# Four reorderings at the stage boundaries of a two-layer mLSTM / Mamba-2 decoder step

## The reference

```
def _conv_ffn(h, buf, w_up, conv_w, conv_b, w_down):
    u = h @ w_up                                  # 2048 -> 2 x 5632
    u, buf_new = _causal_dwconv(u, buf, conv_w, conv_b)   # 3 taps; buf: the old rows
    g, val = jnp.split(u, 2, axis=-1)
    return (jax.nn.silu(g) * val) @ w_down, buf_new       # 5632 -> 2048
```

## Time and profile before

| | |
|---|---|
| three runs | 3429.54, 3431.39, 3434.74 us |
| span of the profiled execution, first to last instruction | 3425.9 us |
| time of the profiled execution as a run | not shown; its span is 5.5 us under the median of the runs |
| TensorE busy | 3279.2 us, 96% |
| VectorE, ScalarE, POOL busy | 2114.1, 1350.2, 887.6 us |
| mean granted TensorE clock | 0.957 of 2.4 GHz |
| DMA | 545.56 MB, 159 GB/s on average |

### The profile page before, as it was taken

One profiled execution on the slowest core, in us unless ns is written; L12 is line 12 of the kernel. 1 busy time (PEld: TensorE's weight loads), 2 busy tenths in 40 slices (PEclk: granted clock), 3 DMA queues, 4 the chain that ended last, 5 costly groups with the idle time before them and its releaser, 6 DMA issues.

```text
span 3425.9 us, 64127 instructions
## 1 busy us (share of the span) xinstructions
PE 3279.2 (96%) x23449; PEld 3192.2 (93%) x23449; DVE 2114.1 (62%) x3198; ACT 1350.2 (39%) x1691; POOL 887.6 (26%) x1123
## 2 busy tenths in 40 slices
PE   7999999999999999989999999999989999999997
PEld 6999999999999999988888988988889999999997
DVE  4554556676546675567676676676666674467644
ACT  4332324444334444443343333343344543344432
POOL 2101013222102232225442343243332230023221
PEclk9999999999999999999999999998899999999999
DMA  5343435444454444544444444444434444544444
GB/s 201 137 164 135 174 114 181 147 169 162 145 173 160 171 159 147 172 166 166 157 157 158 157 163 157 168 158 170 169 119 164 166 156 151 172 168 161 161 148 145
DMA packets 91384, 545.56 MB, mean 159 GB/s; under 512 B 11688, under 2 KB 12528, under 8 KB 43904
## 3 DMA queue, kind: packets, MB, share of 16 engines
q1 hardware_dynamic: 71872, 466.98, 38.6%
q0 software_dynamic: 19392, 76.98, 6.2%
HBM read 510.92 MB, written 32.99 MB: 159 GB/s over the span
## 4 chain that ended last, share of the span: by engine, by line
PE 80%; DVE 8%; issue 6%; ACT 4%; POOL 2%; DMA 0%; DVEq 0%; POOLq 0%; ACTq 0%; SPq 0%
PE ps L388 25%; PE ps L389 24%; PE ps L390 24%; PE ps L395 7%; ACT w_hi L660 2%; DVE w_lo L983 2%; DVE b_u L1312 1%; DVE b_u L1314 1%; DVE b_u L1310 0%; DVE work L1397 0%; DVE sumsq L1392 0%; POOL sumsq L1470 0%; POOL b_xw L1614 0%; DVE b_s L1386 0%; ACT b_out_hi L937 0%
## 5 line engine op out<-in xcount | busy, mean ns | idle before, releaser
L388 PE MATMUL ps<-hn_hi,w_hi 128*128 128x288 f32 x4896 | 1481.3, 303 | 36.9 <-DVE w_lo L983 16.8
L389 PE MATMUL ps<-hn_lo,w_hi 128*128 128x288 f32 x4896 | 1461.8, 299 | 0.0
L390 PE MATMUL ps<-hn_hi,w_lo 128*128 128x288 f32 x4896 | 1456.0, 297 | 0.0
L983 DVE TENSOR_TENSOR w_lo<-w_raw,w_hi 128x2048 fp32r<-128x2048 f32 (+1 forms) x482 | 1045.0, 2168 | 593.3 <-ACT w_hi L660 593.0
L660 ACT ACTIVATE w_hi<-w_raw 128x2048 fp32r<-128x2048 f32 (+1 forms) x482 | 857.7, 1780 | 1145.2 <-PE ps L390 1140.5
L388 PEld LDWEIGHTS ps<-hn_hi,w_hi 128*128 128x128 f32 x4896 | 936.9, 191 | 45.8 <-issue 22.1
L389 PEld LDWEIGHTS ps<-hn_lo,w_hi 128*128 128x128 f32 x4896 | 938.0, 192 | 1.2
L390 PEld LDWEIGHTS ps<-hn_hi,w_lo 128*128 128x128 f32 x4896 | 938.6, 192 | 0.0
L1546 POOL COPY f_new<-f_pad 128x2 f32 x176 | 242.6, 1379 | 1080.9 <-ACT f_u L831 1080.9
L388 PE MATMUL ps<-act_hi,w_hi 128*128 128x288 f32 x1408 | 416.2, 296 | 13.8 <-DVE act_lo L1242 13.8
L389 PE MATMUL ps<-act_lo,w_hi 128*128 128x288 f32 x1408 | 418.0, 297 | 0.0
(11 more groups left out here) (261 smaller groups left out, 3462.2 us busy)
## 6 DMA issues: line engine op xcount, KB each, us to landing
w_raw<-wf_up_in SPq DMA_DIRECT2D x176, 1024.0 KB, 4.8
w_raw<-wf_down_in SPq DMA_DIRECT2D x128, 704.0 KB, 4.0
w_raw<-wb_in_in SPq DMA_DIRECT2D x80, 1024.0 KB, 4.8
w_raw<-wa_in_in SPq DMA_DIRECT2D x48, 1024.0 KB, 4.8
w_raw<-wb_out_in SPq DMA_DIRECT2D x32, 1024.0 KB, 4.8
w_raw<-wa_out_in SPq DMA_DIRECT2D x16, 1024.0 KB, 4.8
b_sT<-b_sT_in POOLq DMA_DIRECT2D x32, 512.0 KB, 4.9
b_s<-b_s_in POOLq DMA_DIRECT2D x32, 512.0 KB, 4.4
```

Of the source, the lines that this page charges most:

```text
L388: nc.tensor.matmul(out, w_hi[:, s, col], hi[:, t, :], start=first and k == 0, stop=False)
L389: nc.tensor.matmul(out, w_hi[:, s, col], lo[:, t, :], start=False, stop=False)
L390: m = nc.tensor.matmul(out, w_lo[:, s, col], hi[:, t, :], start=False, stop=end)
L983: TT(w_lo[:, s, 0:cols], w_raw[:, s, 0:cols], w_hi[:, s, 0:cols].bitcast(F32), ALU.subtract).then_inc(w_low, 1)
```

## The change

It has four parts.

1. **The mean after the first up chunk.** At the start of an FFN, TensorE does up chunk 0 (by `first_project`, tile by tile as `hn_lo` comes) and then the mean. ScalarE takes the root after the split of chunk 2, and VectorE makes `w_lo` of chunk 2 between the add of EPS and the reciprocal. VectorE's memsets of `f_pad` no longer wait for the mean. TensorE's loop over the halves is written out, as are the first four up chunks; ScalarE and VectorE write out the first two pairs.
2. **The first two down tiles alternate halves.** The order of the first down chunks of each half is tile 0 first part, tile 1 first part, tile 0 second part, tile 1 second part, on SyncE, TensorE and VectorE alike. The wait for all hidden tiles moves to the third chunk. ScalarE's code of the down part stays.
3. **The old rows load ahead of the squares.** POOL waits for the mixer's stores and issues the load of `f_old` in `residual`, before the memset of `sumsq`, instead of after the mean.
4. **The gate waits follow a projection.** TensorE waits for the gate columns after the first projection of the second head or group.

The core of the diff:

```diff
+FIRST_DOWN = ((0, 0), (1, 0), (0, 1), (1, 1), (2, 0), (2, 1), (3, 0), (3, 1))
+DOWN = ((0, 0), (0, 1), (1, 0), (1, 1), (2, 0), (2, 1), (3, 0), (3, 1))
...
                             load(Count(c0 + j, (h, C_FHALF), (i, 2)), up[h * (2 * FH) + i * 2 + j], CH)
-                    with sp.Fori(0, KT) as i:
+                    for n, (j, q) in enumerate(FIRST_DOWN):
+                        load(Count(c0 + 2 * FH + n, (h, C_FHALF)), down[h * (2 * KT) + (2 * j + q)], DCH)
+                    with sp.Fori(0, KT - 4) as i:
                         for j in range(2):
-                            load(Count(c0 + 2 * FH + j, (h, C_FHALF), (i, 2)), down[h * (2 * KT) + i * 2 + j], DCH)
+                            load(Count(c0 + 2 * FH + 8 + j, (h, C_FHALF), (i, 2)), down[h * (2 * KT) + i * 2 + (8 + j)], DCH)
...
                     if mixed is not None:
+                        if j == 0 and u.base == 1:
+                            pe.wait_ge(ga_done, 1)
                         a_mix(mixed, 1 - p, j)
...
             m.then_inc(ga_turned, 1)
-            pe.wait_ge(ga_done, 1)
             a_head(Count(1), 1, Count(0))
...
             def ffn(layer, c0, n0, ea0, ed0, k):
-                norm(k)
-                with pe.Fori(0, 2) as h:
-                    with pe.Fori(0, FH // 2) as i:
-                        for j in range(4):
-                            wait(pe, proj_taken, Count(ea0 + j - 3, (h, 2 * FH), (i, 4)))
-                            if j == 0:
-
-                                gemm(Count(c0 + j, (h, C_FHALF), (i, 4)), (n0 + j) % 4, hn_hi, hn_lo, range(KT),
-                                     each=lambda t: wait(pe, hn_lo_ready, k * KT + t + 1))
-                            else:
-                                gemm(Count(c0 + j, (h, C_FHALF), (i, 4)), (n0 + j) % 4, hn_hi, hn_lo, range(KT))
-                    wait(pe, f_alo, Count(layer * FT + FH // 2, (h, FH)))
+                def up_four(h, i, first=False):
+                    for j in range(4):
+                        wait(pe, proj_taken, Count(ea0 + j - 3).add(h, 2 * FH).add(i, 4))
+                        c, bank = Count(c0 + j).add(h, C_FHALF).add(i, 4), (n0 + j) % 4
+                        if first and j == 0:
+                            first_project(c, bank, k)
+                            norm(k)
+                        else:
+                            gemm(c, bank, hn_hi, hn_lo, range(KT))
+
+                def down_four(h, i, order):
+                    for n, (j, q) in enumerate(order):
+                        if q == 0:
+                            wait(pe, res_added, Count(ed0 + j - 3).add(h, KT).add(i, 4))
+                        elif order is FIRST_DOWN and j == 0:
+                            wait(pe, f_alo, Count(layer * FT + FH).add(h, FH))
+                        gemm(Count(c0 + 2 * FH + n).add(h, C_FHALF).add(i, 8), (n0 + 2 * FH + j) % 4,
+                             act_hi, act_lo, range(q * FH // 2, (q + 1) * FH // 2), q == 0, q == 1)
+
+                def half(h, done):
+                    with pe.Fori(0, FH // 2 - done) as i:
+                        up_four(h, i if done == 0 else i + done)
+                    wait(pe, f_alo, Count(layer * FT + FH // 2).add(h, FH))
                     pe.sem_inc(pe_passed, 1)
-                    with pe.Fori(0, KT // 4) as i:
-                        for j in range(4):
-                            wait(pe, res_added, Count(ed0 + j - 3, (h, KT), (i, 4)))
-                            for q in range(2):
-                                if j == 0 and q == 1:
-                                    wait(pe, f_alo, Count(layer * FT + FH, (h, FH)))
-                                gemm(Count(c0 + 2 * FH + 2 * j + q, (h, C_FHALF), (i, 8)), (n0 + 2 * FH + j) % 4,
-                                     act_hi, act_lo, range(q * FH // 2, (q + 1) * FH // 2), q == 0, q == 1)
+                    down_four(h, 0, FIRST_DOWN)
+                    with pe.Fori(0, KT // 4 - 1) as i:
+                        down_four(h, i + 1, DOWN)
+
+                up_four(0, 0, True)
+                half(0, 1)
+                half(1, 0)
 
...
                     if mixed is not None:
+                        if j == 0 and u.base == 1:
+                            pe.wait_ge(gb_done, 1)
+                            pe.wait_ge(gb_low, 1)
                         b_mix(mixed, 1 - p, j)
                     elif j == 9:
                         gate_columns_b()
-                if mixed is None:
-                    pe.wait_ge(gb_done, 1)
-                    pe.wait_ge(gb_low, 1)
...
+                            if first_pair and j == 0:
+                                norm(k)
                             if j == 1:
...
 
-                    with act.Fori(0, FH // 2) as i:
+                    if h == 0:
+                        pair(0, 0, True)
+                        pair(0, 1)
+                    with act.Fori(0, FH // 2 - (h == 0)) as i:
                         for par in range(2):
-                            pair(i, par)
+                            pair(i + 1 if h == 0 else i, par)
...
-                norm(k)
                 half(0)
                 half(1)
 
...
                 TT(w_lo[:, s, 0:cols], w_raw[:, s, 0:cols], w_hi[:, s, 0:cols].bitcast(F32), ALU.subtract).then_inc(w_low, 1)
 
-            def norm(k):
+            def norm(k, between=None):
 
                 wait(dve, mean_ready, k + 1)
                 TS_(rstd[:], ps[:, M0, 0:T], EPS, None, ALU.add).then_inc(var_ready, 1)
+                if between is not None:
+                    between()
...
 
-                def four(i, tail):
-                    for j in range(4):
-                        for q in range(2):
-                            ahead = tail and j == 3
-                            if q == 1:
-                                wait(dve, chunk_done, c0.plus((j + 1) * 2).add(i, 8))
-                                t = Count(j).add(i, 4).value
-                                TT(x[:, t, :], x[:, t, :], ps[:, (n0 + j) % 4, 0:T], ALU.add).then_inc(res_added, 1)
-                            if not (ahead and last):
-                                split(c0.plus(j * 2 + q + 2).add(i, 8), CH if ahead else DCH)
-                        if k is not None:
+                def four(i, tail, order=DOWN):
+                    for n, (j, q) in enumerate(order):
+                        ahead = tail and j == 3
+                        if q == 1:
+                            wait(dve, chunk_done, c0.plus(n + 1).add(i, 8))
+                            t = Count(j).add(i, 4).value
+                            TT(x[:, t, :], x[:, t, :], ps[:, (n0 + j) % 4, 0:T], ALU.add).then_inc(res_added, 1)
+                        if not (ahead and last):
+                            split(c0.plus(n + 2).add(i, 8), CH if ahead else DCH)
+                        if q == 1 and k is not None:
                             input_low(k, Count(j).add(i, 4))
-                with dve.Fori(0, KT // 4 - 1) as i:
-                    four(i, False)
+                four(0, False, FIRST_DOWN)
+                with dve.Fori(0, KT // 4 - 2) as i:
+                    four(i + 1, False)
                 four(KT // 4 - 1, True)
 
...
                     dve.wait_ge(b_new_out, 16 * B_GROUPS)
-                wait(dve, mean_ready, k + 1)
                 for s in range(4):
                     V.memset(f_pad[:, s, 0:2], 0.0).then_inc(f_conved, 1)
...
-                    def pair(i, par):
+                    def pair(i, par, first_pair=False):
                         m = Count(first // 2 + par).add(h, FH).add(i, 2)
                         for j in range(2):
                             s = 2 * par + j
                             n = Count(s).add(h, 2 * FH).add(i, 4)
                             c = Count(c0 + s).add(h, C_FHALF).add(i, 4)
+                            ahead = first_pair and j == 0
+                            if ahead:
+                                norm(k, lambda: split(c.plus(2)))
                             wait(dve, chunk_done, c.plus(1))
                             wait(dve, f_prefix, n.plus(first + 1))
                             src = ps[:, (c0 + s) % 4, 0:T]
                             TT(f_pad[:, s, 2:2 + TP], src[:, 0:TP], rstd[:, 0:TP], ALU.mult)
                             TT(f_samples(f_pad[:, s, :])[:, :, 2:], packed(src), packed(rstd), ALU.mult).then_inc(proj_taken, 1)
-                            split(c.plus(2))
+                            if not ahead:
+                                split(c.plus(2))
...
-            def residual(norms, sq0, used=None):
+            def residual(norms, sq0, used=None, layer=None):
 
                 until(mean_ready, norms)
                 if used is not None:
                     until(*used)
+                if layer is not None:
+                    mixed_out(layer)
+                    pool.dma_start(f_old[:], d["f_old"][layer]).then_inc(f_old_in, 16)
```

(32 more changed lines are left out.)

5 lines of the change are left out of this document (2 added, 3 removed).

## The result

Four runs of the changed kernel gave 3382.93, 3385.39, 3388.31 and 3393.57 us: a median of **3386.85 us**, against 3431.89 for four runs of the kernel before on the same chip. The ratio is 0.9875 (0.986 to 0.9889), so the change takes 45 us off.

What follows compares the result with a forecast made beforehand. TensorE, busy 96% of the span, was taken as the bound, its idle stretches as the gain: 13.8 + 13.8 - 1.2 + 2.25 + 6.9 = 35.6 us, so 3431.4 - 35.6 = 3395.8 us. Range: 3390 to 3405.

Steps and rivals of the forecast that it cites:

- FFN starts: Both places where an FFN begins: up chunk 0 runs without waiting for the mean, saving 6.9 us each, 13.8 together.
- Turns: The four passages from up to down: the wait for `act_lo` goes, saving 3.4, 3.4, 3.5 and 3.5 us, 13.8 together.
- the new wait: At each passage from up to down, TensorE idles about 1.4 us for the third chunk's `w_lo`, clock taken as held.
- The give-back: In second halves, tile 0's square delays the split of down chunk 4: 0.6 us lost in layer 0, 0.2 in layer 1.
- the 0.1 a turn for `w_lo` of chunk 1: At each passage from up to down, a loss of 0.1 us, as that `w_lo` ends at 883.14 against 883.23 wanted.
- Gates: Waits for gate columns, moved behind a projection: 2.25 us saved at the second mLSTM head, 6.9 at Mamba's second group.
- lent-gates rival: In the mixers, the 9.1 us saved at the gate waits returns as longer waits for `b_dec`: 3404.9 us, chance 0.07.
- Old rows: POOL's earlier 704 KB load of `f_old`, ahead of its squares: taken to gain or lose zero.
- The bound of 0.5: In layer 0, an out chunk's weight load queued wholly behind the 704 KB load would be 0.5 us too long.
- Instruction starvation: Rival: written-out chunks leave TensorE short of instructions, up to 1.52 us at each of 40 chunks, 3456.6 us; chance 0.03.
- the change touches no matmul: Whole kernel: TensorE is busy 275.87 of 276.00 us in up chunks, so time moves only at idle stretches and what follows.
- what lies around the span doesn't change: The 5.5 us between the profiled span of 3425.9 and the three runs' median of 3431.39 was taken as constant.

Runs made afterwards that it cites:

- the plain order: The changed kernel with the first down chunks back in sequence (tile 0 in both parts, then tile 1): 3402.79 us, ratio 0.9922.
- the repeat: The changed kernel timed once more, unchanged, beside the kernel before: 3386.4 us, ratio 0.9886.
- the gates experiment: The changed kernel with both gate waits back ahead of the second head's and the second group's first projection: 3400.58 us, ratio 0.9909.

## Why the prediction was right, and where it was wrong

**FFN starts: right.** Forecast 6.9 each; measured 7.1 and 7.0 in the pair of profiles, 8.3 and 7.2 by putting the mean back. Chunk 1 was done 14.27 us after the last out chunk instead of 21.03, where 14.2 instead of 21.1 was forecast.

**Turns: right.** 3.4, 3.4, 3.5, 3.5 forecast, 3.50, 3.51, 3.57, 3.57 measured; the new wait 1.11 us instead of 1.4, with the clock held at 1.00, as behind all 28 such waits (1.09 to 1.12 us) in seven profiles. The reason given for that, that the clock had held over 2.25 us at 79, was one sample and luck: it fell behind the same wait in two other profiles. The give-back was 0.53 and 0.10 by the plain order, 0.6 and 0.2 forecast; the 0.1 a turn for `w_lo` of chunk 1 did not show.

**Gates: right at the gates, with a price for the clock missing at the first.** The first wait of 2.25 is gone, but from that head to the last the gain is 0.7, since there the low clock took 54.6 us instead of 51.2, which costs half of the 3.4 (the other 1.1 of the table's 1.8 were gained before the gate, where nothing is changed). Where the clock falls behind the wait, as in two profiles, it costs 3.8 us and not 2.25. At Mamba 7.0 came where 6.9 was forecast. Ahead of it the start of the mixer is 2.0 us longer, 1.05 by the wait on the store and the rest with 3.4 us more at the low clock behind it (in the repeat 1.3 longer); the sum had no term for that. The lent-gates rival did not occur: `b_dec` fell from 28.8 to 27.6.

**Old rows: zero, right**, down to 0.01 us. The bound of 0.5 for it took 4.8 us as the landing time of an out chunk's load, which is the least of the three in the earlier trace rows; the median is 5.4. **Instruction starvation: did not occur**; "issue" kept one wait of 1.6 us, at the loop's jump back of the earlier trace rows.

**What failed, first: "the change touches no matmul", so the time "can only move at the idle stretches and at what follows them".** The up stretches were read as steady, since TensorE is busy in them 275.87 of 276.00 us. They were not at their floor: ScalarE's table load in each pass held back `w_lo` by a little, 0.07 to 0.18 us a pass, which appears hardly at all as idleness (0.14 us against 2.02 lost), because it only widens one or two steps between overlapping matmuls. Writing two pairs out put 2 loads in the place of 22: 2.7 us missing from the sum. Sum in spans: 35.6 forecast, 39.2 measured, and 38.3 with this term.

**Second, and larger: "what lies around the span doesn't change", 5.5 us.** The 5.5 is not around the span. A run takes 1.5 to 1.9 us more than its span, in every execution where both are listed; so the profiled execution of before took, by estimate, 3427.5, and was 3.9 us faster than the median of its runs. The profiled one of after was 1.5 us slower than its own. Of the 8.95 us by which the median was missed, 3.6 are in the spans and 5.35 are this. Some of the 3.9 was the luck of three runs: all 41 timed runs of the kernel before have a median of 3429.54, 1.85 below the 3431.39 of the forecast. The eight runs of the change, with a median of 3386.85, are 42.7 us below that. Part of the distance can be boundaries that cost more in most executions than in the profiled one (1.5 us at the first gate, in two of three profiles that have its wait); one profile of each kernel can't say how much. The range had allowed for 1.9 us of spread between runs, on three runs of before; 17 of them spread over 13.6 us. Had the distance of the profiled execution from the median been taken as unknown and not as fixed, the low end would have been 3390.7 - 3.9 = 3386.8, at the measured time, and with the 2.7 of the loads below it.

**The spread itself** lies in the mixers. Between up chunk 3 and the turn two runs differ by 0.01 us; the mLSTM heads took 395.65 to 402.60 us in twelve profiles, and the difference goes with the time at the low clock. The window of that stretch, before, in the change, and in the gates experiment (51.2, 54.6 and 61.4 us at the low clock):

```profile
76.63:473.00 396.37, 394.12 (x2681) 378.71 (x2681) 200.35 (x290) 125.92 (x196) 39.08 (x34) 0.94 0.42 151
```

```profile
75.54:471.19 395.65, 395.65 (x2681) 380.17 (x2681) 200.41 (x290) 125.96 (x195) 39.08 (x34) 0.93 0.43 151
```

```profile
75.36:476.42 401.06, 398.81 (x2681) 383.31 (x2681) 200.44 (x290) 125.95 (x196) 39.13 (x34) 0.92 0.43 149
```

TensorE is busy throughout in the second, and its clock is still 0.93. What lowers it there I have not tested.

## What to carry to other kernels

When an engine's loop is entered with a state its body doesn't share (here ScalarE's table), look for the load at the top of each pass, even where the bound engine looks 100% busy; one pass written out ended it here. Compare the steps between equal instructions, which show a loss that the busy time hides. When two executions are to be compared by their spans, fix first what a run's time adds to its own span, and keep the distance between the profiled execution and the median as an uncertainty, not as a constant. Look at the waits that a change doesn't aim at too: a memset's wait for a store stood in the trace of before already, and moving the store was worth 6.4 us, nearly as much as one start of an FFN.

## What had not been expected of the hardware

**The fall of the clock isn't a matter of idleness alone.** In the kernel with only the pairs written out TensorE idled 3.41 to 3.43 us at each turn, as before, but the clock fell only at two of the four; there the turn cost 15.72 and 15.63 us, elsewhere 14.22 and 14.23. In the plain-order kernel one such idleness of 3.31 us brought 6.83 us at the low clock instead of 3.41. Behind the first gate wait, of 2.24 or 2.25 us, it fell in two of three profiles. Only behind the 1.1 us of the new turns did it never fall, in 28 cases. The prediction's two readings, "it was 1.00 after the 2.25" and "in each of the four turns it fell", were samples of one and of four.

**A wait for a store can be the longest of a boundary.** VectorE stood 7.80 us for `fconv_out` before, 8.85 after, and 1.99 (and that for TensorE) once the store was issued ahead of POOL's squares.

**A table load costs its 1.28 us and no more.** In the timeline above `act_hi` ends at 654.04, the load starts at 654.09, and the next instruction at 655.38, which is 1.34 us from end to start. The Trainium skill ("ScalarE: Activation LUTs", "What ACT_TABLE_LOAD costs") gives about 1283 ns for the load, and the trace agrees (a mean of 1283 over 23); the drain of about 1380 ns that the page adds to it for every switch isn't there. Its rule to batch calls by set rather than by function bears on this case: the square root ahead of a loop put a load into each of the loop's passes, and there it cost TensorE 0.07 to 0.18 us a pass.
